# Spreading the projection items of a decoder step one to a slot, and prompt attention over 37 slots in place of 43

## What is computed

```python
z = xn @ w_in                                    # conv B | C | x | q | k | v | forget | gates
# prompt: 8 heads x 64, causal, 8 query tiles of 128 tokens
sc = q_tile @ k.T * scale + dcum_q - dcum_k      # decay from the forget gates
out = softmax(causal(sc)) @ v
# sample: each of the 8 sequences attends to 4096 past tokens in pages of 128
sp = q_new @ k_past.T * scale + d_new + rev
sn = q_new @ k_new.T * scale + d_new - d_new
out = softmax([sp, sn]) @ [v_past, v_new]
```

## Time and profile before

| | us |
|---|---|
| median of 3 timed runs | 2039.61 (2038.65 to 2041.22) |
| the profiled execution, its own time | 2033.3 |
| span of its trace | 2031.6 |
| PE busy in the span | 1874.0 (92%) |
| slot 0 begins (PE) | 71.6 |
| slot 28 begins | 269.6 |
| slot 73 ends | 547.1 |

### The profile page before, as it was taken

How to read it: one execution, slowest core, us unless ns; L and a number is a source line. 1 busy time by engine, 2 the same in 40 slices (tenths; PEclk the granted TensorE clock), 3 DMA queues, 4 the chain that set the end, 5 groups by cost and what they waited for, 6 DMA issues and landing times.

```text
span 2031.6 us, 33494 instructions
## 1 busy us (share of the span) xinstructions
PE 1874.0 (92%) x12402; PEld 1109.6 (55%) x12402; DVE 832.0 (41%) x1867; ACT 442.2 (22%) x1021; POOL 250.8 (12%) x381
## 2 busy tenths in 40 slices
PE   6999988888999999999999898994999999999994
PEld 4677655555588868888864466543333333333331
DVE  5644476877666423333353406334111111111115
ACT  3111133434301011111111205231222222212213
POOL 0203233323100000000000000000111111111110
PEclk9999999999999999999999999997999999999997
DMA  7759999999912130210111204038999999999966
GB/s 254 267 176 344 350 353 352 362 347 350 312 39 95 47 119 11 63 52 11 63 65 65 84 1 156 21 119 327 355 383 388 379 371 375 371 371 376 371 222 262
DMA packets 208099, 458.56 MB, mean 226 GB/s; under 512 B 18657, under 2 KB 47354, under 8 KB 207554
## 3 DMA queue, kind: packets, MB, share of 16 engines
q1 hardware_dynamic: 177490, 365.30, 50.1%
q0 software_dynamic: 30448, 91.13, 12.5%
HBM read 432.44 MB, written 32.17 MB: 229 GB/s over the span
## 4 chain that ended last, share of the span: by engine, by line
PE 79%; DVE 7%; DMA 5%; issue 4%; ACT 3%; DVEq 2%; SPq 1%; POOLq 0%; ACTq 0%; POOL 0%
PE ps L1315 17%; PE ps L1625 11%; PE ps L1656 6%; PE ps L1144 6%; PE ps L1380 6%; PE ps L1636 5%; PE ps L1409 5%; PE ps L1665 3%; PE ps L1116 3%; PE ps L1159 3%; PE ps L1498 2%; DMA kraw<-in_cache_k 2%; PE ps L1267 2%; PE ps L1247 2%; DMA vpage<-in_cache_v 2%
## 5 line engine op out<-in xcount | busy, mean ns | idle before, releaser
L1625 PE MATMUL ps<-gu,xgT 128*64 128x512 f32 x1024 | 226.8, 595 | 0.9 <-ACT xgT L1973 0.9
L2156 DVE STREAM_TRANSPOSE kt<-kraw 128x1024 f32<-128x1024 f32 x128 | 151.1, 1218 | 42.4 <-DMA kraw<-in_cache_k 33.2
L1315 PE MATMUL ps<-xnT,ring 128*128 128x264 f32 x672 | 158.8, 387 | 0.8 <-DMA xnT<-xn_d 0.8
L860 POOL DMA_DIRECT2D vpage<-in_cache_v x228 | 122.5, 537 | 290.8 <-PE ps L1267 236.0
L2892 DVE TENSOR_TENSOR sig_a<-ps,sig_a 128x256 f32<-128x256 f32 x32 | 13.6, 425 | 323.4 <-ACT sig_a L1977 323.4
L1625 PEld LDWEIGHTS ps<-gu,xgT 128*64 128x64 f32 x1024 | 70.6, 137 | 131.9 <-issue 128.8
L1315 PEld LDWEIGHTS ps<-xnT,ring 128*128 128x128 f32 x672 | 127.4, 190 | 23.7 <-DMA xnT<-xn_d 1.7
L1656 PE MATMUL ps<-wd,hidT_a 128*64 128x512 f32 x512 | 116.9, 598 | 19.3 <-ACT hidT_a L1983 9.6
L1636 PE MATMUL ps<-gu,xgT 128*32 128x512 f32 x1024 | 115.8, 592 | 0.0
L1144 PE MATMUL ps<-xnT,early 128*128 128x352 f32 x320 | 101.9, 474 | 3.8 <-issue 3.8
L1144 PEld LDWEIGHTS ps<-xnT,early 128*128 128x128 f32 x320 | 61.0, 195 | 37.9 <-issue 8.7
(11 more groups left out here) (444 smaller groups left out, 2909.6 us busy)
## 6 DMA issues: line engine op xcount, KB each, us to landing
kraw<-in_cache_k SPq DMA_DIRECT2D x256, 256.0 KB, 5.0
gu<-in_w_expert_gate SPq DMA_DIRECT2D x32, 2048.0 KB, 20.3
gu<-in_w_expert_up SPq DMA_DIRECT2D x32, 2048.0 KB, 25.0
wd<-in_w_expert_down SPq DMA_DIRECT2D x31, 2048.0 KB, 21.2
vpage<-in_cache_v POOLq DMA_DIRECT2D x228, 256.0 KB, 5.4
ring<-in_w_in SPq DMA_DIRECT2D x12, 1024.0 KB, 8.0
yy<-y_d SPq DMA_DIRECT2D x16, 512.0 KB, 10.2
early<-in_w_in SPq DMA_DIRECT2D x6, 1024.0 KB, 11.7
```

The costliest lines, as they stand in the source:

```text
L860: eng.dma_start(vpage[value_place(n)][:, p, :], t["cache_v"][ds(page, 1)].rearrange("a s d -> (a s) d")).then_inc(v_in[value_place(n)], 16)
L1315: last = nc.tensor.matmul(bank(R.bank(name, f, q))[:, 0:QT], weight[:, k], src[:, k, cols], start=k == 0, stop=k == HK - 1)
L1625: last = nc.tensor.matmul(bank(0)[h * BA:(h + 1) * BA, :].rearrange("p (x n) -> p x n", x=2), src[:, k, 0:BA], weight[:, k, :, h * DE // 2 ...
L2156: last = nc.vector.transpose(kt[n % 2].rearrange("p c e s -> p (c e s)")[:, x * 1024:(x + 1) * 1024], kraw[n % 2].rearrange("p c d -> p (c ...
```

## The change

Each of slots 0 to 33 now takes one item. The order of items changes in one place: the first tile of v's second half comes after five tiles of the first half. Prompt attention goes over slots 35 to 71, 37 slots: 10 with one half and 27 with two, of which 14 hold both halves of one job and 13 cross from one job to the next. The turned keys of the prompt are taken in slots 36 to 44. The new tokens' scores (`new_scores`, `take_new`) move from slot 5 to 6. In SP's list the waits and loads for weights and decay rows stand behind later units.

```diff
-        ITEMS = ([("q", f, n) for f, n in REST] + [("v", half, i) for half in range(2) for i in VTILES]
+        ITEMS = ([("q", f, n) for f, n in REST] + [("v", 0, i) for i in VTILES[:5]] + [("v", 1, PT)]
+                 + [("v", 0, i) for i in VTILES[5:]] + [("v", 1, i) for i in VTILES[1:]]
                  + [("k", f, n) for f, n in REST])
-        PROMPT0, PROMPT_SLOTS, KOUT0 = 29, 43, 30
+        PROMPT0, PROMPT_SLOTS, KOUT0 = 35, 37, 36
 
         def items(n):
 
-            first = n + min((n + 1) // 2, 6)
-            return ITEMS[first:first + (2 if n < 12 and n % 2 == 0 else 1)]
+            return ITEMS[n:n + 1]
...
-            if n == 5:
+            if n == 6:
                 R.add("dve", "snew", banks=TURNS)
                 R.add("dve", "lf", banks=(0, 1, 4))
...
-                if n == 7:
+                if n == 8:
                     R.made(sp, "q", 1, 1)
                     early_load(0, O_V)
-                if n == 9:
+                if n == 12:
                     R.made(sp, "q", 3, 1)
                     early_load(1, O_V)
-                if n == 15:
+                if n == 22:
                     R.made(sp, "v", 0, PT - 1)
                     early_load(0, O_K)
-                if n == 24:
+                if n == 31:
                     R.made(sp, "v", 1, PT - 1)
                     early_load(1, O_K)
-                if n == 28:
+                if n == 34:
                     R.made(sp, "k", 1, 1)
                     sp.wait_ge(neg_stored, 16)
                     load_negk(0)
-                if n == 35:
+                if n == 40:
                     R.made(sp, "k", 3, 1)
                     sp.wait_ge(xn_stored, 16)
                     load_negk(1)
```

## The result

The changed kernel is slower: 2049.6 us against 2040.1 (medians of four runs each), ratio 1.0054 with a 95% interval of 1.0038 to 1.0071. Timed again beside later experiments it had 1.0045 (1.0028 to 1.0063). The prediction, 2038.0 within 2027 to 2047.5, missed on the slow side.

A forecast was written before the change was run, and what follows sets the result against it. The loop was taken as bound by PE's work and its waits inside prompt attention. Terms 2.2 + 1.0 - 6.3 + 1.0 + 0.5 = -1.6 us gave 2031.7 profiled, 2038.0 us timed, range 2027 to 2047.5.

The forecast's parts named there:

- slot 1's wait: With one item in slot 0, PE waits in slot 1 for ACT to empty bank 5: +2.2 us.
- v slots' data: Slots 10 to 27: 35.7 MB for 16 v slots arrive almost hidden behind PE's work at about 380 GB/s: +1.0 us.
- PE's waits in the jobs' slots: Prompt attention: -6.3 us for late data, +1.0 for waits on ACT and DVE, +0.5 at the loop's end.
- Slots 10 to 27: one item each, as before, but more v: Sixteen v slots in a row: their data is hidden but for 0.7 us at 380 GB/s, taken as +1.0 us.
- a rival with 0.09 and +3.9 for the whole: The v slots run out of data: +6.5 us in place of +1.0, total 2043.5 us; chance 0.09.
- The signs by which the forecast would be wrong: `vpage` waits in v slots over 4 us, or `diag` and `probT` waits together over 40 or under 22 us.
- A DMA share of 0.97 looks like a bound and is nearly none: Slots 28 to 62: loads mostly land in time; of PE's 39.3 us of waits from slot 28, 5.6 are on values.
- The jobs' own waits: Prompt attention: PE's waits for ACT and DVE between matmuls, 31.7 us before, change by +1 us, between -4 and +9.
- -8 for batch ends: Prompt attention: four batch ends (41, 49, 57, 65) in place of five, two in slots with a single half: about -8 us.
- The rival of denser jobs: Prompt attention: each two-half slot keeps 1.5 us of waits, +9.1 in place of +1, total 2046 us; chance 0.18.
- SP's later waits: SP's loads of weights and decay rows behind later units still land in time, three slots being 21 us: no cost.
- The offset: The profiled execution lies 6.3 us below the median of the timed runs, and this was taken to stay.

The follow-up runs named there:

- the second profile: The changed kernel profiled and timed again, nothing changed: ratio 1.0045 to the kernel before, loop 487.8 us; the kernel before was also profiled again unchanged, loop 478.0 us.
- whole jobs: Slots with two halves take both from one job, single halves at batch ends: kernel before, 43 slots, 1.0026; changed kernel, 37 slots, 0.9996.
- the best version: Changed kernel with whole jobs over 37 slots, two items in slot 0, k's halves loaded behind units 24 and 29: ratio 0.9993, 2036.8 us.

## Why the prediction was wrong

By its own steps, for the first profile of each; the loop got 17.1 us longer where I had -1.6:

| step | predicted | measured |
|---|---|---|
| slot 1's wait | +2.2 | +2.2, and 1.7 at the lower clock (not in the second profile) |
| v slots' data | +1.0 | +6.4 of waits, 2.6 at the lower clock behind them |
| slot 34 | 0 | +1.0 |
| PE's waits in the jobs' slots | -4.8 | -4.4 (38.8 to 34.4 us) |
| PE's busy time there | 0 | +6.5 (235.0 less 13.6 of the slots that left, to 228.0) |
| spread over the item slots | 0 | +1.1 |

The sum is 17.1. Between the second profiles of the two kernels the loop grew by 9.8 us: the item slots lost 13.4 us (15.0 in the table), the jobs' waits fell by 4.6 us, and their busy time rose by 1.1 us only. So the loss of the item slots is sure, and so is the saving in the jobs' waits; how much the clock takes back there is partly chance.

**The step that failed first is "Slots 10 to 27: one item each, as before, but more v", "I take +1.0".** The waits were 6.4 us, 1.0 on values and 5.5 on keys, and 2.6 us of lower clock stood behind them. I took 380 GB/s from the middle of a stretch whose mean was 358, and held that against PE's mean. The kernel before does hold 378 over its slots 12 to 18, 42 us, but no run holds it over 16 v slots. Slots 10 to 19 ran at 357 GB/s, and slots 10 to 25 at 345 in the changed kernel and at 366, the most of any version with these 16 v slots, in the one with the later load, whole jobs and two items in slot 0:

```profile
135.70:238.90 103.20, 96.76 (x1033) 68.91 (x1032) 49.71 (x95) 14.14 (x45) 32.58 (x61) 0.97 0.97 345
135.80:234.30 98.50, 95.54 (x1029) 67.12 (x1028) 49.02 (x95) 14.38 (x45) 32.43 (x61) 1.00 1.01 366
```

By the best of these rates the 35.7 MB take 97.5 us, a term of +4.3, and by the mean of 358 +6.5. The Trainium skill ("DMA: Bandwidth & Descriptors", Specifications) gives about 358 GB/s for a core, which made the same estimate of +6.5 for this term. This trace agrees in size, as the waits came to 6.4 us, but the runs do not bear out 358 as a limit: 366 GB/s over 98.5 us is above it. The waits were 5.4 us in the second execution and 4.3 with the load later, so a part of the match is luck. The experiment without the 1 MB load shows that this load is what the v slots cannot take; the one with a later load shows that its place is about a third of the wait. The mechanism was named as a rival with 0.09 and +3.9 for the whole. The signs by which the forecast would be wrong looked elsewhere: waits on `vpage` in the v slots were 1.0 us, under the 4 that were set, and those on `diag` and `probT` 27.4 us, between 22 and 40. The keys, which DVE turns first, had no sign.

**The clock had no term at all.** I counted PE's work as the same before and after, and it is, but its busy time grew by 12.5 us, as the trace has 41 us at 1.2 GHz in place of 10. In the jobs' slots the predicted saving in waits came (-4.4) and was taken back by busy time (+6.5), in the second profiles by +1.1 only. Waits on the sums were fewer and longer: 6 in place of 10, and 4.4 us is the longest, against 2.3. That the longer ones bring the lower clock fits both places shown above, but was not tested by itself.

**"A DMA share of 0.97 looks like a bound and is nearly none" was half true.** PE's waits name ACT and DVE, but when whole jobs took 22 us of waits for sums and copies away in the kernel before, 16.5 us on data and 10.4 us on maxima came in their place and it got slower. A limit by data stood close behind the other, in that deal at least, and the view of waits names only the one that came last.

**The jobs' own waits** were sized right in sum and wrong in kind: I booked -8 for batch ends that now meet single halves, by the slots behind the ends (41, 49), and overlooked that the ends themselves (40, 48, 56) meet crossings, 12.2, 14.4 and 11.8 us long. The rival of denser jobs, each pair at 1.5 us and +9.1, did not come: the item slots are what lost. (Slots 35 to 63 hold 51 halves and not 50, as slots 29 to 62 did; the argument stays the same.)

**SP's later waits** cost nothing here, but "three slots are 21 us" was too generous: the load was issued in slot 28 and not 27, since unit 31's keys wait for DVE, and it landed 13.3 us later, just in time. With the need one slot sooner it cost 6.8 us, and with whole jobs over 37 slots PE waited 1.2 us for it.

**The offset** between profile and timed median, 6.3 us, did not stay: the profiled execution after lies 0.6 us under its median. Beside the second profile of the changed kernel it was 6.1 us above the median. So of the 15.7 us between the spans, the timed runs show 8 to 11.

What stays open: why a wait is followed by the lower level in one execution and not in another, how many of the jobs' 6.5 us a larger number of profiles would show, and how much of slots 33 and 34's wait for values in the best version could be won by placing the decay rows elsewhere, which was not tried.

## What to carry to other kernels

When a stream runs near its limit, size a denser stretch by the mean rate over a whole stretch of the same kind, not by its best slices, and look at what stands in the same queue ahead of the loads that someone waits for. Waits that name an engine may cover for data that would be late right behind them: before taking them away, see what comes next. And count a new wait of PE at more than its length, since the work behind it may run at half the clock. Here, in the jobs' slots, 34 us of waiting with longer waits on the sums came with more time at that level than 39 us with shorter ones.

## What was not expected of the hardware

- A v item took 5.3 us behind a PE wait of 5.5 us, against 3.7; 41 and 31 us of lower clock in the loop of two executions of the changed kernel, 10 and 17 in two of the kernel before, with PE 91 to 92% busy in all four.
- Two executions of the changed kernel have the waits of the item slots alike (2.24 and 2.23, 5.45 and 5.43), while their loops differ by 4.8 us, most of it in busy time, where the clock was lower. Waits in the jobs' slots vary more: those on the inverted sums were 12.1 and 9.6 us in two executions of the kernel before. Behind the loop, where nothing was changed, the two executions of the changed kernel took 1484.2 and 1490.4 us.
- 1 MB more in a stretch of 16 slots that was already full cost 7 to 9 us, some three times the 2.9 us that it takes at 358 GB/s.
- The DMAs kept 366 GB/s over 98.5 us in the v slots of the best version, and 345 over 103.2 us in those of the changed kernel, in which keys stood behind a burst in their queue.
